# Decode samples' key products moved into the projection's value blocks; down-projection passage and merge entry reordered

## What is computed

```python
def conv_ffn(x, hist, g, w_up, cw, cb, w_down):
    u = jnp.einsum('btd,df->btf', rms_norm(x, g), w_up)          # 1024 -> 2 * 2816
    ext = jnp.concatenate([hist, u], axis=1)
    c = cb + sum(cw[j] * ext[:, j: j + T] for j in range(3))     # three taps
    a, b = jnp.split(c, 2, axis=-1)
    return jnp.einsum('btf,fd->btd', silu(a) * b, w_down), ext[:, -2:]

def dilated_sample(q, k_buf, v_buf, k_new, v_new, dil, n_back):   # a decode sample, one head group
    # kg, vg: every dil-th row of the sample's own K/V cache, then its new row
    s = jnp.einsum('bthe,btkhe->bthk', q, kg)
    lse = logsumexp(s); p = exp(s - lse)
    return jnp.einsum('bthk,btkhe->bthe', p, vg), lse

# mixer: softmax over the three groups' lse weighs their outputs; then w_o
```

## Time and profile before

| | us |
|---|---|
| median of 3 runs | 2199.49 |
| lowest, highest | 2195.18, 2202.12 |
| time of the profiled execution | 2197.47 |
| its span, first to last instruction | 2195.7 |
| PE busy in it | 2139.5 (97%) |
| DVE, ACT, POOL busy | 1534.3, 979.4, 480.6 |
| mean granted clock of PE | 0.987 |

### The profile page before, as it was taken

The page is one execution under the profiler, slowest core; times in us unless marked ns, Lnnn a source line. Parts: engine busy times, 40 slices in busy tenths (PEclk is TensorE's granted clock), DMA queues, the critical chain, the costliest instruction groups (busy, mean ns, idle before and its releaser), DMA issues.

```text
span 2195.7 us, 42914 instructions
## 1 busy us (share of the span) xinstructions
PE 2139.5 (97%) x15928; PEld 2005.8 (91%) x15939; DVE 1534.3 (70%) x2375; ACT 979.4 (45%) x1854; POOL 480.6 (22%) x674
## 2 busy tenths in 40 slices
PE   7999999999999999999999999799999999999998
PEld 7999999999999977777777788599999999999998
DVE  4888888887556677365463678678888888775554
ACT  4655554555445532122121445456555545554332
POOL 1002223323100155154252120010122233221000
PEclk8999999999999999999999999899999999999999
DMA  6236777788985522223222688541467788899664
GB/s 192 86 97 181 188 205 199 189 208 229 300 258 183 169 96 82 97 82 101 97 102 100 223 282 250 168 137 59 144 171 199 209 202 195 198 256 309 207 198 144
DMA packets 244623, 383.73 MB, mean 175 GB/s; under 512 B 21624, under 2 KB 118552, under 8 KB 242599
## 3 DMA queue, kind: packets, MB, share of 16 engines
q1 hardware_dynamic: 207878, 284.69, 39.7%
q0 software_dynamic: 31328, 92.66, 19.5%
q10 hardware_dynamic: 5288, 4.68, 0.6%
HBM read 304.10 MB, written 174.43 MB: 218 GB/s over the span
## 4 chain that ended last, share of the span: by engine, by line
PE 88%; DVE 5%; DMA 4%; ACT 2%; issue 1%; POOL 0%; SPq 0%; ACTq 0%; DVEq 0%; POOLq 0%
PE ps L1247 38%; PE ps L1343 19%; PE ps L2096 6%; PE ps L2098 6%; PE ps L2097 6%; PE ps L2344 2%; PE ps L2759 2%; DMA gneg<-gn 1%; PE ps L2317 1%; PE ps L417 1%; PE ps L2328 1%; DMA kc<-in_cache_kv_w 1%; PE ps L858 1%; PE ps L482 1%; PE ps L2284 1%
## 5 line engine op out<-in xcount | busy, mean ns | idle before, releaser
L1247 PE MATMUL ps<-hT,w 128*128 128x258 f32 x2752 | 458.4, 283 | 1.5 <-ACT acc L1173 1.0
L1247 PEld LDWEIGHTS ps<-hT,w 128*128 128x128 f32 x2752 | 385.2, 190 | 2.0 <-ACT acc L1173 1.2
L1247 PE MATMUL ps<-lT,w 128*128 128x258 f32 x1376 | 276.5, 282 | 0.0
L1247 PE MATMUL ps<-hB,w 128*128 128x258 f32 x1344 | 230.5, 283 | 4.4 <-DVE ub L1461 4.4
L2096 PE MATMUL ps<-wq,xh 128*128 128x512 f32 x576 | 227.7, 395 | 0.8 <-DVE wq L1919 0.8
L2098 PE MATMUL ps<-wq,xl 128*128 128x512 f32 x576 | 227.4, 395 | 0.0
L2097 PE MATMUL ps<-wq,xh 128*128 128x512 f32 x576 | 226.9, 394 | 0.0
L1247 PEld LDWEIGHTS ps<-lT,w 128*128 128x128 f32 x1376 | 213.6, 190 | 0.0
L1343 PE MATMUL ps<-gdh,wda 128*128 128x258 f32 x1184 | 198.9, 283 | 1.8 <-DVE gdl L1550 1.8
L1247 PEld LDWEIGHTS ps<-hB,w 128*128 128x128 f32 x1344 | 191.8, 190 | 4.8 <-DVE ub L1461 4.8
L1343 PE MATMUL ps<-gdh,wdb 128*128 128x258 f32 x1152 | 193.4, 284 | 0.0
(11 more groups left out here) (346 smaller groups left out, 4797.2 us busy)
## 6 DMA issues: line engine op xcount, KB each, us to landing
stage<-in_w_up SPq DMA_DIRECT2D x176, 256.0 KB, 3.8
wsum<-in_w_down POOLq DMA_DIRECT2D x132, 256.0 KB, 5.3
gs<-cb SPq DMA_DIRECT2D x44, 516.0 KB, 6.7
stage<-wsum SPq DMA_DIRECT2D x88, 256.0 KB, 2.9
tsum<-gs POOLq DMA_DIRECT2D x66, 258.0 KB, 7.5
tsum<-gneg POOLq DMA_DIRECT2D x66, 258.0 KB, 8.1
stage<-in_w_down SPq DMA_DIRECT2D x58, 256.0 KB, 3.1
stage<-in_w_kv SPq DMA_DIRECT2D x24, 512.0 KB, 3.9
```

Source lines behind the costliest of these rows:

```text
L1247: mm = pe.matmul(ps[:, bank + c, 0:HB], w, m[:, c * HB:(c + 1) * HB], start=(first and i == 0), stop=(i == len(parts) - 1), skip_group_che ...
```

## The change

Three parts.

1. The samples' scores are made in the projection. After the rotary of a group, POOL itself issues the loads of the cached keys (`skc`, in `acc`) and of the query (`sqb`, in `rb`), two slots each, and multiplies in place. DVE's reduction `sample_scores` stands behind the value rows of tiles 2 to 8. SP's loads `load_sample` and the 24 reductions of the attention stage are gone. `sc`, `kvt0` and the masks get other places in memory.
2. The passage. In the last feature tile, PE makes the first quarter of down step 0, then P4, then P3. DVE and ACT split step 0 earlier, normalise `ub` before `ua`, and take taps of `b` before those of `a`; step 2 joins steps 0 and 1 before the fourth column block; the low parts of steps 4 to 6 stand between the last taps. In every tile, tap `a` no longer waits until the kept tile is stored.
3. The merge. SP loads groups 0 and 1 of row tiles 0 and 1 before attention ends, and group 2 by itself behind the last store. The second product with `diag`, all four pieces of w_o and the samples' matmuls come before tile 0.

The core of the diff:

```diff
@@ PE, last feature tile and pe_down
-                if not last:
+                if last:
+                    pe.wait_ge(f_dl, S.dl + 2)
+                    pe.wait_ge(f_cp, copied(S, f, "C11"))
+                    pe_down_part(pe, 0, 0, False)
+                    pe.wait_ge(f_cp, copied(S, f, "U3"))
+                    pe_product(pe, S, w12[:, 0, AL], w12[:, 1, AL], "T4", 2, False)
+                    pe.wait_ge(f_cs, 2 * f + (S.cs + 1))
+                    pe_product(pe, S, w24[:, 0, AL], w24[:, 1, AL], "B22", 4, False)
+                else:
                     p1(f + 1)
...
-            ready(0)
-            for d in range(3):
+            for d in range(1, 3):
                 free(0, d)
                 one(0, d, False)
             ready(1)
             for d in range(3):
                 one(1, d, False)
             pe_conv_tails(pe, S, TAILS[NF, 0])
+            ready(2)
+            for d in range(3):
+                one(2, d, False)
             free(0, 3)
-            one(0, 3, False).then_inc(f_dn, 1)
-            one(1, 3, False).then_inc(f_dn, 1)
+            for n in range(3):
+                one(n, 3, False).then_inc(f_dn, 1)
@@ DVE, last feature tile
                 dve_tap(v, L, S, f - 1, 0, 1)
                 dve_tap(v, L, S, f - 1, 1, 1)
+                if last:
+                    dve_down(v, S, 0)
                 dve_tap(v, L, S, f - 1, 0, 0)
...
-            dve_norm(v, S, ua, 0, f)
             dve_norm(v, S, ub, 1, f)
             dve_down(v, S, 2)
-            dve_tap(v, L, S, f, 0, 1)
-            dve_tap(v, L, S, f, 1, 1)
+            dve_c12(v, S, f)
+            dve_norm(v, S, ua, 0, f)
+            dve_tap(v, L, S, f, 1, 1, True)
             dve_down(v, S, 3)
-            dve_tap(v, L, S, f, 0, 0)
-            dve_tap(v, L, S, f, 1, 0)
+            dve_tap(v, L, S, f, 1, 0, True)
+            dve_tap(v, L, S, f, 0, 1, True)
+            dve_down(v, S, 4)
+            dve_tap(v, L, S, f, 0, 0, True)
+            dve_down(v, S, 5)
             dve_prod(v, S, f)
+            dve_down(v, S, 6)
@@ ACT, tap
                     act.wait_ge(f_prod, f + S.prod)
-                    act.wait_ge(f_kept, 32 * f + S.kept)
+                    if h:
+                        act.wait_ge(f_kept, 32 * f + S.kept)
@@ DVE, value blocks
+            def sample_scores(g, s, last):
+                rows = KEYS[GROUPS - 1] if last else KEYS[0]
+                v.wait_ge(sm_p, NS * g + s + 1)
+                nc.vector.tensor_reduce(sc[0:rows, bass.ds(g * 64 + s * 8, HEADS)],
+                                        skc[s % 2][0:rows, :].rearrange("p (h e) -> p h e", h=HEADS), AX.X,
+                                        ALU.add).then_inc(sm_r, 1)
+
...
+                            if t >= 2:
+                                sample_scores(g, t - 2, last)
+                            if t == 8:
+                                sample_scores(g, 7, last)
@@ POOL, after each group's rotary
+            def load_keys(g, s):
+                n = NS * g + s
+                if n >= 2:
+                    q.wait_ge(sm_r, n - 1)
+                q.dma_start(skc[s % 2][0:KEYS[g], :], a[CACHES[g]][s, ::DIL[g], 0].rearrange(
+                    "t h e -> t (h e)")).then_inc(sm_k[s % 2], 16)
+
+            def load_query(g, s):
+                q.dma_start(sqb[s % 2], qs[g, T + s, :].partition_broadcast(P)).then_inc(sm_q[s % 2], 16)
...
+                load_keys(g, 0)
+                load_keys(g, 1)
+                q.wait_ge(rows_out[2], 16 + 144 * g + 16 * (6 if g < GROUPS - 1 else 9))
+                load_query(g, 0)
+                load_query(g, 1)
+                for s in range(NS):
+                    n = NS * g + s
+                    q.wait_ge(sm_k[s % 2], 16 * (n // 2 + 1))
+                    q.wait_ge(sm_q[s % 2], 16 * (n // 2 + 1))
+                    nc.gpsimd.tensor_tensor(skc[s % 2][0:KEYS[g], :], skc[s % 2][0:KEYS[g], :], sqb[s % 2][0:KEYS[g], :],
+                                            ALU.mult).then_inc(sm_p, 1)
+                    if s + 2 < NS:
+                        load_keys(g, s + 2)
+                        load_query(g, s + 2)
@@ SP, end of attention and merge
+                if s == NSTEP + 1:
+                    for i in range(3):
+                        sp.wait_ge(rows_out[i], ROWS + moved(15 - (15 - i) % 3, 3))
+                    sp.wait_ge(at_tp, 2 * NSTEP - 1)
+                    sp.wait_ge(at_o, 2 * NSTEP - 2)
+                    for t in range(2):
+                        load_merged(sp, t, 0, 2)
...
+            sp.wait_ge(wo_l, 1)
+            load_wo(sp, 3)
+            sp.wait_ge(at_o, NH)
             for i in range(3):
                 sp.wait_ge(rows_out[i], ROWS + moved(NSTEP - 3 + i, 3))
...
+                if t >= 2:
+                    load_merged(sp, t, 0, 2)
+                load_merged(sp, t, 2, 3)
@@ DVE, merge
-            for k in range(3):
+            dve_diagonal(v, 1)
+            for k in range(4):
                 split_wo(k)
+            samples()
             first(0)
```

More of the change, by code:

```diff
@@ L1407, in kept_by @@
         def kept_by(q):
-            return max(2 * (i % NF) + i // NF + 1 for i in range(NP * q, NP * q + NP))
+            return 2 * NF if q % 2 else max(2 * (i % NF) + i // NF + 1 for i in range(NP * q, NP * q + NP))
         def tail_out(q):
@@ L1675, in act_downs @@
         def act_downs(act, S):
-            for n in range(4, NSTEPS):
+            for n in range(7, NSTEPS):
                 act_down(act, S, n)
@@ L1720, in tap, with silu @@
                                      u[:, T:2 + N], ACT.Copy).then_inc(f_ut, 1)
[L1722 to L1723 removed]
+            def silu(f, taps=6):
+                act.wait_ge(f_conv, 8 * f + (S.conv + taps))
                 nc.scalar.activation(ca[:, :], ca[:, :], ACT.Silu).then_inc(f_silu_ng, 1)
@@ L1766, in act_ffn @@
             act_copy_c21(act, S, f)
+            act_down(act, S, 2)
+            tap(f, 1, 1)
+            act_down(act, S, 3)
             tap(f, 0, 1)
-            tap(f, 1, 1)
             act_conv_tails(act, L, S, TAILS[NF, 0])
-            silu(f)
+            act_down(act, S, 4)
+            silu(f, 8)
+            act_down(act, S, 5)
+            act_down(act, S, 6)
             negated(f, 1)
@@ L2038, in pool_project @@
             half = HEADS * 8
-            with q.Fori(0, GROUPS) as g:
+            def load_keys(g, s):
[6 more added lines that the diff above has]
+                q.dma_start(sqb[s % 2], qs[g, T + s, :].partition_broadcast(P)).then_inc(sm_q[s % 2], 16)
+            for g in range(GROUPS):
                 for u in (0, 1):
@@ L2706, in act_merge @@
                 split_wo(k)
+            act.wait_ge(sm_st, 14)
+            split_wo(3)
+            samples()
             for t in range(8):
@@ L2777, in pe_merge @@
             pe.wait_ge(at_oc, NH)
+            pe.wait_ge(sm_st, 14)
+            for c in range(4):
+                cols = slice(c * P, (c + 1) * P)
+                for i, m in enumerate((om1, om2)):
+                    out = ps[:, 5, c * NS + 4 * i:c * NS + 4 * i + 4]
+                    pe.matmul(out, m[:, cols], selS, start=True, stop=False)
+                    mm = pe.matmul(out, onew[:, cols], ident[0:NS, 4 * i:4 * i + 4], start=False, stop=True)
+            mm.then_inc(sm_f, 1)
             for t in range(8):
```

143 lines of the change are left out of this document (46 added, 97 removed).

## The result

| | us |
|---|---|
| before: median of 4 runs | 2199.42 (2195.18 to 2202.12) |
| changed: median of 4 runs | 2186.61 (2184.53 to 2189.37) |
| ratio, 95% interval | 0.9944, 0.9925 to 0.9964 |
| profiled execution of the changed kernel, its span | 2189.37, 2187.6 |
| PE busy in it | 2141.6 (98%) |

The account below looks back on a forecast made before the run. PE was taken as the bound almost everywhere. Passages 8.8, attention 2.0, projection 0 and merge 2.5 made 13.3 us off the profiled 2197.47, so 2184.2; as a median 2186, range 2177 to 2196.

Parts of the forecast that it names:

- the 0.98: Second passage: PE's 0.98 us wait for ACT's copy goes, as tap a no longer waits for the kept tile.
- 16 matmuls would have taken 1.95 us instead of 3.0, 1.05 us back: First passage: the low clock after the wait for `dve_c22` goes with that wait, giving 1.05 us.
- 0 us, bounds 0 and +3: Projection and attention's start: the moved sample scores make nothing late for PE, 0 us, bounds 0 and +3.
- 5 us later, at 1217.31: Attention's start: after ending the projection at 1211, PE still waits for SP's load of Q, 3.51 us idle.
- that rival: Value blocks: POOL's load issues locked out by DVE, 3.1 us each, estimate 2198; slow issues alone 2 of 9%.
- The 4.9 us of small matmuls move into PE's 13 us hole: Merge: the samples' 32 matmuls fill PE's idle time, so `turn(2)` starts up to 3.85 us earlier.
- my own sign of being wrong: Merge entry: the prediction is wrong if `first(0)` comes later than 9 us behind attention's last output.
- What sets the end is DVE's turns: Merge: DVE's turns behind tile 4's load end at 1449.3 instead of 1451.75, a gain of 2.5 us.
- The passages' half return: Passages: step 0's operands come late and steps 4 to 6 wait for taps; 4.4 us less gain, 2190.6, 12%.
- The fourth piece: Merge entry: the last w_o piece lands in 9.2 us and holds the entry, costing 5.0 us, 2191, 10%.
- The value-block rival: Projection, attention's start: late sample loads eat the gain, 2200 (9%); from 13.8 us per two samples, slower, 2209 (7%).
- The lower end of the range, 2177: Whole kernel: lowest predicted median, from larger gains in passages, attention and merge plus 2 us of scatter.

Follow-up runs that it names:

- One slot: The changed kernel with one slot instead of two for the value blocks' keys and query, each sample's loads waiting for the previous reduction: 2231.55 us, 1.0147.
- P3 first: The changed kernel with P3 ahead of P4 again in the last feature tile, the rest of the new passage order kept: 2194.14 us, 0.9989.
- the product behind the copy: The changed kernel with POOL's last sample product waiting for DVE's copy of the samples' value row: 2185.33 us; with further edits, 2184.95 and 2183.58.
- the lean entry: The changed kernel with the fourth w_o piece and the samples' high and low parts split before row tile 4, not ahead of tile 0: 2186.24 us, 0.9945.

## Why the prediction was right, and where it was wrong

The stages, first row to first row on PE (the projection to its last row's end), over all executions that share a stage's code. One slot is not among them, nor are the other kernels where their edit acts. In the kernel before, the projection's first row on PE stands at 771.50, not at 765.

| stage | old code (executions) | new code (executions) | mean change | forecast |
|---|---|---|---|---|
| ConvFFN 0 to step 4, less low-clock time | 472.1, 472.2, 472.1 (3) | 467.6 to 468.9 (9) | -3.9 | -4.4 |
| merge's end to step 4 of layer 1, likewise | 470.7, 468.7, 469.5 (3) | 465.4 to 467.3 (9) | -3.2 | -4.4 |
| projection | 439.7 to 439.9 (3) | 439.6 to 440.2 (10) | 0 | 0 |
| attention, half-steps 0 to 4 | 16.2, 16.4, 17.0 (3) | 17.4 to 19.6 (7) | +1.5 | 0 |
| attention, half-steps 16 to 36 | 78.6, 78.9, 79.8 (3) | 77.0 (10) | -2.1 | -2.0 |
| attention's last output to the end of turn(7) | 44.1, 44.5, 44.6 (3) | 41.2 to 43.6 (7) | -2.1 | -2.5 |

The sum is -9.8 us against 13.3 forecast. The medians say 12.8 and 13.0, with intervals from 7.9 and 9.2 on. So the median fell where I put it, but the stages carry only three quarters of it.

The other 3 us can be narrowed down by the span and the granted clock on record for every execution. Over 52 executions of the kernel before and 10 of the changed one the mean span falls from 2196.6 to 2184.8 us, 11.8 and not 12.8. Span times clock, the time as it would be at full clock, falls from 2166.9 to 2156.6, that is by 10.3 and near the stages' sum. The remaining 1.5 us are low-clock time, 29.7 against 28.2 us, with a standard error of 0.9. Over all kernels with the new passages (53 executions, without P3 first and one slot) it is 27.3 us, over all with the old ones (76) 29.5, and with P3 first, where the passages' waits are back, 30.2 (12); the error of such a mean is 0.3 to 0.7. So part of what the time gained is less time at the lower clock. Where it lies the fourteen profiles don't show, and its cause stays open.

**Passages: the mechanism was right, the size was not: 8.8 us was 7.1 by the stages, 5.9 in the passages themselves.** The waits went as told: 1.57 to 2.25 (mean 1.9) + 0.42 + 0.89 = 3.2 us before, 0.2 to 0.8 after, in every execution. From the end of P7 to step 4 a passage took 21.2 to 21.9 us without low-clock time in the old code and 18.3 to 19.0 in the new, 3.0 less in layer 0 and 2.9 in layer 1. The other 1.2 us of the table lie in the feature loops ahead, where of the booked terms only the 0.98 stands, and are in part made by taking the low-clock time off: in layer 0 the same loop took 450.5 us in three executions without such a stretch, and 449.3 after the subtraction in five of six with one. The step that was mis-sized is the sum of a single profile's waits. Two of its terms did not come in every execution. "16 matmuls would have taken 1.95 us instead of 3.0, 1.05 us back" took the clock of 0.50 as a sure consequence of the wait; with waits of 2.25, 1.57, 1.84, 1.73 and 1.70 us the five other old passages ran at 1.00. With P3 first, one of two had a stretch at 0.50. That makes two of eight passages with such waits and none of the twenty new ones, so the term is worth a quarter of what was booked, if that. Elsewhere in the ConvFFNs such stretches stand in old and new executions alike, 0 to 3.4 us of low-clock time in each. And the wait of 0.98 for ACT's copy came in one of three old executions; undoing the edit that I credited with it changed nothing there.

**Attention: the reductions gave 2.1 us as forecast, the start took back 1.5.** The step that failed is "0 us, bounds 0 and +3": I followed the reductions and the maxima, which came in time (9.4 us behind tile 7's row, 10.4 booked), and left the samples' row copy at the 0.47 us that it took alone. POOL's product and memset hold it. In the three kernels with the product behind the copy the stage takes 16.4 to 17.2 us, 1.2 less in the mean. (The prediction's "5 us later, at 1217.31" is 5.9, as PE's last row of the projection ends at 1211.39.) The Trainium skill, SBUF — State Buffer (SBUF: two separate sides), says that GpSimd and a DVE instruction in a two-port mode, or with two inputs in SBUF while GpSimd reads SBUF, take one pair of ports for a whole instruction, and that the one that starts first has it while the other waits. Six of the seven held copies agree, and one does not (last section). I had weighed that page for the other direction, the descriptors of POOL's transfers, where it gives 3.1 us in place of 0.62 for a transfer. No issue here took over 0.60, so that rival was rightly low, and the short copy in the path to Q was overlooked.

**Merge: 2.1 us for 2.5, by other steps.** "The 4.9 us of small matmuls move into PE's 13 us hole" is what gives the gain (moved back, the merge is 3.1 us longer than the mean of 42.3). But they run at half the clock there and hold `first(0)` by 1.18 us, so that it came 9.7 us behind the last output. By my own sign of being wrong, later than 9, the account of the entry failed; over the seven executions it is 8.3 to 10.0. "What sets the end is DVE's turns" holds only up to `turn(4)` in the changed kernel: DVE ends 2.3 us sooner, and behind 1435.00 PE's turns with w_o between them set the end. (The forecast's own numbers, 1431.3 and four and three quarter turns, give 1449.15 and not 1449.3.)

**The rivals.** The passages' half return didn't come. The fourth piece landed 3.7 us after its issue, so its rival, a landing in 9.2, didn't come either; DVE's wait of 2.64 us for it was part of the forecast's own sum, and freeing the entry of it gave at most 0.6 us there, since `om` lands no sooner. The value-block rival was priced by the one-slot run: its price was right at attention's start and too low in the projection, and its condition (13.8 us for two samples) was far off, as two samples turned in 7.9 to 8.0 us where nothing but the slots held them.

**The luck in it.** The median met 2186 within 1 us although the start of attention was booked 1.5 us too well and the passages 1.7 to 2.9: less time at the lower clock than in the kernel before (1.5 us in the mean, barely clear of its error) made up for part of it, and the forecast had that only as 1.05 us in one passage. The lower end of the range, 2177, doesn't follow from its terms, which give 2186 - 0.7 - 1.5 - 2.0 - 2.0 = 2179.8.

## What to carry to other kernels

A wait, or a stretch at the lower clock, in one profile can be booked in full only if a second execution of the same code shows it too; here one of ten terms came in one execution of three, and another in two passages of eight. Work moved beside another engine must be checked against the short operations there that a transfer waits for, not only for its own length. And work moved into an idle gap of PE is paid there at the clock of the gap; it is free only while nothing waits for its result.

## What was not expected of the hardware

- A DVE `tensor_scalar` of 8 x 512 floats from SBUF to SBUF took 0.47 us alone and up to 1.84 beside POOL's product and memset. In six of the seven executions where it was held in the last group it ends 0.27 or 0.28 us behind POOL: in three behind the memset, with POOL's durations unchanged, and in three behind the product, where the memset then takes 1.01 us instead of 0.73. Here in group 0 of the changed kernel (DVE, then POOL), 918.00 - 917.73 = 0.27 us, as 1209.06 - 1208.79 above:

```profile
917.01 0.99 DVE L2035 TENSOR_SCALAR kn<-sq,rtok 8x512 f32<-8x512 f32 x1
```

```profile
916.44 1.29 POOL L2118 TENSOR_TENSOR acc<-acc,rb 128x512 f32<-128x512 f32 x1 [2.03 <-DMA rb<-qs]
```

- It goes the other way as well, and then both are longer: in the kernel with the lean entry POOL's product began 0.05 us behind the copy and took 2.20 us instead of 1.26, while the copy, which had started first, took 1.14 (DVE, then POOL). If the first one simply had the ports for itself, it would have kept its 0.47 us. It was seen once.

```profile
1205.43 1.14 DVE L2035 TENSOR_SCALAR kn<-sq,rtok 8x512 f32<-8x512 f32 x1
```

```profile
1205.48 2.20 POOL L2118 TENSOR_TENSOR acc<-acc,rb 64x512 f32<-64x512 f32 x1 [2.40 <-DMA rb<-qs]
```

- POOL's issue of a load took 0.53 to 0.60 us in the projection, where its weight-sum transfers of the earlier trace rows took 0.8 to 1.5. What makes the difference stays open.
- In PE's gap behind attention the 32 small matmuls ran at a granted clock of 0.50 to 0.53 (0.50 is 1.2 GHz) for 8.0 us although they followed each other at once, and took 6.5 to 8.3 us in ten executions; in the kernel before they ran behind two turns, at 1.00, and took 4.9 us.
